# One hybrid attention and expert layer on one core: router logits inside the output projection, rows gathered per 32-slot block of an expert, two more weight buffers, and the heads' remainders on VectorE instead of GpSimd

## The reference, cut to what matters

```python
x = x + merged @ w_out[i]
h = rms_norm(x, ffn_norm[i])
group_logits = h @ w_group + b_group          # 4 groups, top 1
exp_logits   = h @ w_router + b_router        # 8 experts in each, top 2 in the group
# every token goes to 2 of 32 experts
hid = silu(xb @ w_gate[e]) * (xb @ w_up[e])   # 2048 -> 512
y   = hid @ w_down[e]                         # 512 -> 2048
x = x + weighted sum of the two experts' rows
x = x + sigmoid(rms_norm(x, ple_norm[i]) @ w_ple_gate[i]) * (p[i] @ w_ple_proj[i])
```

## Time and profile before

| | us |
|---|---|
| median of 3 runs | 2308.14 |
| lowest and highest | 2308.02, 2311.95 |
| profiled execution, its own time | 2307.7 |
| its span on the core | 2306.2 |
| mean granted TensorE clock | 0.926 of full |
| TensorE busy | 1815.4 (79%) |
| VectorE busy | 859.9 (37%) |
| ScalarE busy | 698.6 (30%) |
| GpSimd busy | 377.2 (16%) |
| DMA, mean over the span | 257 GB/s, 593 MB |

### The profile page before, as it was taken

How to read it: one execution, slowest core, us unless ns; L and a number is a source line. 1 busy time by engine, 2 the same in 40 slices (tenths; PEclk the granted TensorE clock), 3 DMA queues, 4 the chain that set the end, 5 groups by cost and what they waited for, 6 DMA issues and landing times.

```text
span 2306.2 us, 40236 instructions
## 1 busy us (share of the span) xinstructions
PE 1815.4 (79%) x17038; PEld 1428.8 (62%) x17039; DVE 859.9 (37%) x1284; ACT 698.6 (30%) x952; POOL 377.2 (16%) x120
## 2 busy tenths in 40 slices
PE   5899999999987999999896776665556566655689
PEld 5688888888875888888775443333333333333367
DVE  1454465435533454544445322222222122222264
ACT  3355455544554343334331110000000000000063
POOL 7454454535443000000001000000000000000000
PEclk9999999999998999999996898888898888889899
DMA  7444434443422555555571899999999999999973
GB/s 155 110 129 127 109 103 115 110 120 97 109 92 82 192 193 190 193 191 194 202 291 46 347 426 424 426 427 426 426 426 426 426 426 426 426 426 427 426 289 108
DMA packets 256837, 593.05 MB, mean 257 GB/s; under 512 B 29450, under 2 KB 168970, under 8 KB 223242
## 3 DMA queue, kind: packets, MB, share of 16 engines
q1 hardware_dynamic: 256778, 592.19, 68.8%
HBM read 590.06 MB, written 2.10 MB: 257 GB/s over the span
## 4 chain that ended last, share of the span: by engine, by line
PE 48%; DMA 36%; DVE 6%; ACT 4%; DVEq 2%; ACTq 2%; issue 1%; POOL 1%; SPq 0%
DMA ring<-in_w_e_down 34%; PE bank L662 20%; PE bank L469 12%; PE bank L870 4%; PE bank L812 3%; DVEq L1242 2%; DVE ring L1367 1%; PE bank L587 1%; DVE mo L1361 1%; ACT ring L924 1%; ACT wh L924 1%; DMA ring<-in_w_in 1%; ACT L924 1%; PE bank L787 1%; PE bank L590 1%
## 5 line engine op out<-in xcount | busy, mean ns | idle before, releaser
L787 PE MATMUL bank<-ring,mo 128*32 128x128 f32 x8192 | 327.8, 327 | 262.6 <-DMA ring<-in_w_e_gate 131.4
L787 PEld LDWEIGHTS bank<-ring,mo 128*32 128x32 f32 x8192 | 282.3, 132 | 345.5 <-DMA ring<-in_w_e_gate 167.5
L924 ACT ACTIVATE wh<-ring 128x2048 fp32r<-128x2048 f32 x156 | 298.5, 1913 | 266.6 <-DMA ring<-in_w_in 143.1
L405 POOL TENSOR_TENSOR wl<-ring,wh 128x2048 fp32r<-128x2048 f32 x68 | 314.3, 4632 | 312.5 <-ACT wh L924 312.5
L1609 DVE TENSOR_TENSOR x_tok<-x_tok,bank 128x512 f32<-128x512 f32 x256 | 158.7, 681 | 497.0 <-PE bank L776 497.0
L469 PE MATMUL bank<-xh,wh 128*128 128x256 f32 x1088 | 292.0, 304 | 9.0 <-POOL xl L411 9.0
L924 ACT ACTIVATE mo<-bank 128x256 f32<-128x256 f32 (+3 forms) x201 | 68.2, 348 | 749.7 <-PE bank L799 338.1
L469 PE MATMUL bank<-xl,wh 128*128 128x256 f32 x1088 | 274.1, 288 | 0.0
L1436 DVE TENSOR_TENSOR wl<-ring,wh 128x2048 fp32r<-128x2048 f32 x80 | 183.3, 2292 | 232.7 <-ACT wh L924 232.7
L469 PEld LDWEIGHTS bank<-xh,wh 128*128 128x128 f32 x1088 | 213.5, 196 | 15.9 <-POOL xl L411 9.2
L469 PEld LDWEIGHTS bank<-xl,wh 128*128 128x128 f32 x1088 | 214.2, 197 | 2.4 <-issue 1.9
(11 more groups left out here) (337 smaller groups left out, 2278.7 us busy)
## 6 DMA issues: line engine op xcount, KB each, us to landing
ring<-in_w_e_down SPq DMA_DIRECT2D x64, 2048.0 KB, 26.7
ring<-in_w_e_gate SPq DMA_DIRECT2D x64, 2048.0 KB, 24.0
ring<-in_w_e_up SPq DMA_DIRECT2D x64, 2048.0 KB, 26.1
ring<-in_w_in SPq DMA_DIRECT2D x116, 1024.0 KB, 5.5
ring<-in_w_out SPq DMA_DIRECT2D x16, 1024.0 KB, 5.2
ring<-in_w_ple_gate SPq DMA_DIRECT2D x8, 2048.0 KB, 14.5
ring<-in_w_branch_a SPq DMA_DIRECT2D x8, 1024.0 KB, 5.1
ring<-in_w_branch_b SPq DMA_DIRECT2D x8, 1024.0 KB, 5.2
```

The lines of the kernel that those rows point to most:

```text
L405: pool.tensor_tensor(wl[p][:], slot[p], wh[p][:], ALU.subtract).then_inc(sem("w_lo"), 1)
L787: m = mm(bank[b][32 * j:32 * j + 32, 0:P], xw[:, 8 * (i % 2) + k, :], m_gu[i][:, k, j * P:j * P + P], start=(i % 2 == 0 and k == 0), stop= ...
L924: return act.activation(out, in_, func, **kw)
```

## The change

1. **Remainders.** GpSimd keeps only the first two tiles' remainders and `xl`. All others go to VectorE, as `lo(p, t)`, one at a time at fixed places in its lists (in `mix` after `decT`, after `sp`, after `eG`, in rounds 1 and 3, before the chunks, in chunk 1, and after the head). The long stand of ScalarE in the last head is shortened: high parts of units 6 and 7 come after it.
2. **Start.** TensorE waits for `xh` instead of `xl`, products with `xl` come second in a tile; `gc` and the eight diagonal products go between head 0's dense quarters.
3. **Router logits.** While block n of the output projection runs, block n-1 of the new x is transposed, scaled by `ffn_norm` (`ngr`, a further small load) and multiplied with the router's weights; the root is applied to the logits afterwards. `h_tok` is made by ScalarE.
4. **Gather.** No `sel`, `xs`, `h_hi`, `h_lo`. Each window begins with eight float32 products of its own 32 selected slots (`selw`) with `h_rows`, an evacuation `xg`, four transposes and `xw`.
5. **Buffers.** The freed space makes two more gate buffers; gate pieces of even and odd experts alternate. Expert 1's gate pieces and `wpp` are loaded before the first window; loads of experts 0 and 1 start at units 78 to 84.

The diff, cut to its core:

```diff
-            base[f"plfull{b}"] = (f"mfull{b}", 16 * NE)
+            base[f"plfull{b}"] = (f"mfull{b}", 16 * (NE // 2 if b < 2 else NE))
...
+        xg = mo[:, 8192:8704]
+        x1T = [mo[:, 8192 + 1024 * i:9216 + 1024 * i].rearrange("p (k s) -> p k s", k=4) for i in range(2)]
...
+        m_flat += [xnT[:, :, :].rearrange("p t s -> p (t s)").rearrange("p (a n) -> p a n", a=1),
+                   mo[:, 4096:8192].rearrange("p (a n) -> p a n", a=1)]
...
+                if u in (78, 80):
+                    i = 4 + (u - 78) // 2
                     sp.wait_ge(*event("mT_lo", 8))
+                    expert_piece(i, 0).then_inc(sem(f"mfull{i}"), 16)
+                if u in (82, 84):
+                    i = (u - 82) // 2
+                    sp.wait_ge(*event("unit_mm", NG_U))
+                    expert_piece(i, 1, 1).then_inc(sem(f"mfull{i + 6}"), 16)
+            for i in (0, 2, 1, 3):
+                sp.wait_ge(*event("unit_mm", NU - 2 + 2 * (i % 2)))
                 expert_piece(i, 0).then_inc(sem(f"mfull{i}"), 16)
-            sp.wait_ge(*event("gathered", KT))
-            sp.dma_start(wpp[:], wpp_v).then_inc(sem("wpp_in"), 16)
-            with sp.Fori(1, NE) as e:
-                for i in range(6):
-                    sp.wait_ge(*event(f"mused{i}", e))
-                    expert_piece(i, e).then_inc(sem(f"mfull{i}"), 16)
+            sp.dma_start(wpp, wpp_v).then_inc(sem("wpp_in"), 16)
+            for i in range(2, 6):
+                sp.wait_ge(*event(f"mused{i}", 1))
+                expert_piece(i, 1).then_inc(sem(f"mfull{i}"), 16)
+            with sp.Fori(1, NE // 2) as h:
+                for odd in range(2):
+                    for i in range(6):
+                        sp.wait_ge(*event(f"mused{i}", 2 * h + odd - (1 if i < 2 else 0)))
+                        expert_piece(i, 2 * h + odd, odd).then_inc(sem(f"mfull{i + 6 * odd if i < 2 else i}"), 16)
...
-                steps = [(wh[p], x_, k) for k in range(KT) for x_ in (xh, xl)] + [(wl[p], xh, k) for k in range(KT)]
+                steps = [(w_, x_, k) for w_, x_ in ((wh[p], xh), (wh[p], xl), (wl[p], xh)) for k in range(KT)]
...
-            pe.wait_ge(*event("x_lo", 8))
+            pe.wait_ge(*event("x_hi", 8))
...
+            for q in range(4, 32):
+                dense(0, q)
+                if q % 2 == 1 and q // 2 - 2 < 8:
+                    i = q // 2 - 2
+                    pe.wait_ge(*event("diag", i + 1))
+                    if i >= 2:
+                        pe.wait_ge(*event("diag_bc", i - 1))
+                    mm(bank[4 + i % 2][:], ones[:], (cv if i % 2 == 0 else ex)[:, 0:512], start=True, stop=True)\
+                        .then_inc(sem("diag_mm"), 1)
...
-            pe.wait_ge(*event("head", NH + 1))
+            pe.wait_ge(*event("dn_ort", NH))
...
+                    if n and j == 1:
+                        x1_transposes(n - 1)
+                    if n and j == 2:
+                        part_logits(n - 1)
+            x1_transposes(3)
+            pe.wait_ge(*event("lT", 1))
             for t in range(TT):
+                pe.wait_ge(*event("x1T", 7 + t))
+                logits = bank[7][:, t * 36:t * 36 + 36]
+                mm(logits, lT[:, t * P:t * P + P], ident[0:NG + NE, 0:NG + NE], start=True, stop=False)
+                for k in range(4):
+                    m = mm(logits, x1T[1][:, k, t * P:t * P + P], wr[:, 12 + k, :], start=False, stop=(k == 3))
...
+            def window(v, gate_full, full, odd, last):
+                pe.wait_ge(*event("selw", v))
+                pe.wait_ge(*event("hidden", v))
+                for t in range(TT):
+                    for j in range(4):
+                        m = mm(bank[0][32 * j:32 * j + 32, :], selw[:, t, :], h_rows[:, t, 512 * j:512 * j + 512],
+                               start=(t == 0), stop=(t == 1))
+                m.then_inc(sem("xg_mm"), 1)
+                combine(v, 0).then_inc(sem("c_mm"), 1)
+                pe.wait_ge(*event("xg", v))
+                for q in range(4):
+                    m = pe.transpose(bank[1][:, q * P:q * P + P], xg[:, q * P:q * P + P], ident[:])
+                m.then_inc(sem("xw_mm"), 1)
                 pe.wait_ge(*event("xw", v))
...
-                if s in (2, 3, 5, 6, 7, 8):
+                if s in (2, 3, 5, 6):
                     unit_hi(s if s < 4 else s - 1)
             mix(NH, lambda s: None, first_units, lambda: None)
+            unit_hi(6)
+            unit_hi(7)
...
+            def lo(p, t):
+                dve.wait_ge(*event("w_hi", t + 1))
+                tt(wl[p][:], slot[p], wh[p][:], ALU.subtract).then_inc(sem("v_lo"), 1)
+            lo(2, 2)
+            lo(3, 3)
             dve.wait_ge(*event("small_in", 16 * SMALL))
...
                 tt(eG, eG, qk_dn[:, 0:S], ALU.mult).then_inc(sem("decays_used"), 1)
+                lo(4)
...
                     if r < 4:
                         next_tap(r)
+                    if r in (1, 3):
+                        lo(5 + r // 2)
...
                 next_silu()
+                lo(7)
                 for c in range(NCH):
...
+                    if c == 1:
+                        lo(8)
...
             def window(v, c):
-                dve.tensor_copy(xw, xs[:, :, ds(c, WIN)]).then_inc(sem("xw"), 1)
+                for t in range(TT):
+                    i = ts(selw[:, t, :], iota[:, ds(c, WIN)], pw[:, t:t + 1], None, ALU.is_equal)
+                i.then_inc(sem("selw"), 1)
                 add(v, 0)
+                dve.wait_ge(*event("xw_mm", v))
+                tt(xw.rearrange("p (j q) s -> p q j s", j=4), bank[1][:].rearrange("p (q j s) -> p q j s", q=4, j=4),
+                   bc(ngf[:].rearrange("p (j q) -> p q j", j=4).unsqueeze(3), [P, 4, 4, WIN]), ALU.mult)\
+                    .then_inc(sem("xw"), 1)
```

More of the change, by code:

```diff
@@ L787, in window @@
                             m = mm(bank[b][32 * j:32 * j + 32, 0:P], xw[:, 8 * (i % 2) + k, :],
-                                   m_gu[i][:, k, j * P:j * P + P], start=(i % 2 == 0 and k == 0),
+                                   m_gu[piece][:, k, j * P:j * P + P], start=(i % 2 == 0 and k == 0),
                                    stop=(i % 2 == 1 and k == 7))
@@ L823, in expert @@
                     with pe.Fori(0, more) as w:
-                        window(w0 + w + 1, e1 * 16, False)
-                window(w0 + more + 1, e1 * 16, True)
+                        window(w0 + w + 1, gate_full, full, odd, False)
+                window(w0 + more + 1, gate_full, full, odd, True)
             def ple_part(n):
@@ L835, in _ @@
             pe.wait_ge(*event("jobs", 1))
-            expert(0, 1)
+            pe.wait_ge(*event("h_tok", 2))
             pe.wait_ge(*event("pT", 1))
             pe.wait_ge(*event("wpp_in", 16))
-            ple_part(0)
-            with pe.Fori(1, 4) as e:
-                expert(e, e + 1)
-                ple_part(e)
-            with pe.Fori(4, NE) as e:
-                expert(e, e + 1)
+            with pe.Fori(0, 2) as h:
+                for odd in range(2):
+                    expert(h, odd)
+                    ple_part(2 * h + odd)
+            with pe.Fori(2, NE // 2) as h:
+                for odd in range(2):
+                    expert(h, odd)
             more = pe.value_load(jobs[0:1, 0, NE - 1:NE], min_val=0, max_val=7)
@@ L988, in _, with decay_rows @@
                 .then_inc(sem("gc_exp"), 1)
-            for i in range(0, 8, 2):
+            def decay_rows(i):
                 act.wait_ge(*event("diag_mm", i + 1))
@@ L1464, in x1_add, with x1_evac @@
                     tt(o, o, bank[2 * (n % 2) + t][:], ALU.add).then_inc(sem("x1"), 1)
+            def x1_evac(n):
+                for t in range(TT):
+                    dve.wait_ge(*event("x1T_in", 2 * n + t + 1))
+                    if n == 2:
+                        dve.wait_ge(*event("lT_part", 1))
+                    if n == 3:
+                        dve.wait_ge(*event("lT_part", 2))
+                    tt(x1T[n % 2][:, :, t * P:t * P + P], bank[4 + t][:].rearrange("p (k n) -> p k n", k=4),
+                       bc(ngr[:, 4 * n:4 * n + 4].unsqueeze(2), [P, 4, P]), ALU.mult).then_inc(sem("x1T"), 1)
             for b in range(3):
@@ L1477, in _ @@
                     x1_add((u - 79) // 4)
+                if u in (81, 85):
+                    x1_evac((u - 81) // 4)
                 unit_lo(u)
+            x1_evac(2)
             x1_add(3)
-            dve.wait_ge(*event("x1_rms", 1))
-            for t in range(TT):
-                ts(h_tok[:, t, :, :], x_tok[:, t, :].rearrange("p (c k) -> p k c", k=KT), rs2[:, 4 + t:5 + t], None,
-                   ALU.mult).then_inc(sem("h_tok"), 1)
-            evac_T(xnT, "hT", ngf)
+            x1_evac(3)
             dve.wait_ge(*event("logits", 1))
@@ L1489, in _ @@
             b8 = lambda i, w: bc(rsm[:, i, :].unsqueeze(2), [P, TT, w])
-            lp = bank[6][:, 0:72].rearrange("p (t n) -> p t n", t=TT)
```

(4 more changed lines are left out.)

217 lines of the change are left out of this document (98 added, 119 removed).

## The result

The changed kernel is slower: 2402.93 us (median of 4 runs, 2400.93 to 2411.28) beside 2309.1 (2308.02 to 2311.95), a ratio of 1.0411 (95% interval 1.0384 to 1.0439). Faster by 54 us was forecast. The profiled execution was the slowest of the four, with a span of 2409.3 us.

The account below looks back on a forecast made before the run. DMA was taken to bound the expert stage and TensorE nearly the heads, with a DMA hole between. Terms 1 to 5 summed as -8 +2 -8 +8 -47.5 = -53.5, thus 2254 us; range 2228 to 2282.

Parts of the forecast that it names:

- Term 5: Last output unit to expert 1's loads: first buffer free at U+40, +4 for early holes, later gather hidden; -47.5 us.
- three signs: Heads off by over 3 us each, a period above 29.5 after four experts, or TensorE awaiting DMA between output units.
- the rivals: Heads gain fully, 2216 us (0.10); early windows decide, 2271 (0.13); remainders on path, 2340 (0.04); DMA starts late, 2275 (0.02).
- the slower one: Seven loop heads: all 18.3 us of VectorE's remainders a head come on the path, +88 instead of +2, 2340 us; chance 0.04.
- Term 2: Seven loop heads: long VectorE rows vanish, new waits cost +6, steadier clock gives -4; +2 us in all.
- no wait of that length is left: -4: Seven loop heads: without the 3.3 us wait, the lower clock's loss of about 1 us in some heads goes.
- Terms 1, 3 and 4: Start, earlier dense tiles: -8 us; last head, gate products sooner: -8; output projection, added transposes and router products: +8.
- its 7 us: Early expert windows: the second, 3.4 us pause lowers the clock, costing 1.7 us more each, 7 in all, none later.

Follow-up runs that it names:

- one copy: Changed kernel with TensorE's second copy of the window code, for experts of more than one window, left out: 2263.93 us, 0.9804 of the kernel before.

## Why the prediction was wrong

The marks, in us; "heads" is from the second turn of the loop to the last head (VectorE's copy of `hs`), "branch" the first product with `oh`, U the end of the last output unit, "freed" SyncE's first load that waits for window 0, "last" the last half of the down products. "GpSimd" is one copy with the remainders back on GpSimd.

| stretch | before | changed | one copy | GpSimd | forecast |
|---|---|---|---|---|---|
| start to second turn | 211.37 | 207.32 | 204.26 | 204.91 | -8 |
| six turns | 456.4 | 467.4 | 464.2 | 458.2 | +2 |
| last head to branch | 89.5 | 80.2 | 80.0 | 78.6 | -8 |
| branch to U | 447.1 | 456.2 | 456.1 | 456.3 | +8 |
| U to freed | 77.4 | 40.8 | 37.3 | 37.4 | 40 |
| freed to last | 921.3 | 1054.4 | 912.3 | 915.5 | 911.2 |
| last to end | 103.2 | 103.0 | 103.0 | 103.0 | same |

**Term 5 failed, in its last part.** "Windows without `ple_part` need some 21 us of 29.5; there the gather is hidden under DMA" counted instructions and their durations, and not that the same loop was now twice as long in code. The 21 us were right (20.5 measured); the window began to cost more when it could no longer stay where TensorE runs it from. From the freed buffer to the last down products 1054.4 us passed instead of 911.2, and with one copy 912.3. The last down products came at 2306.3, 156.8 us after the forecast's 2149.5 (a span of 2252.7 less 103.2): 143.2 of it in this stretch, 12.8 up to U and 0.8 between. By the medians the code is worth 139. The rest of the term held: the buffer free at U+40.8 (forecast U+40; U+37.3 without a fetch ahead of window 0), and the last half at U+949.6 with one copy (forecast 951.2). Two of its figures don't follow from their own terms: 19.7, 2, 885 and 4 are 910.7 and not 911.2, and 24.45 with at most 2.0 and 3.4 is 29.9 and not 31.4. Neither matters beside 143.

Of the three signs I had named for a wrong forecast, one decided, "a period above 29.5 after the first four experts", and I had no mechanism for it. None of the rivals held it either: the slower one had its place in the heads. What was in sight before: the loops over experts in the diff, two experts a turn instead of one, and the number of packets on q8.

**Term 2 was mis-sized.** +2 for the heads; six turns measured +11.0 in the changed kernel and +7.8 with one copy. VectorE's long rows went, as forecast: the row that took 4.08 us is L1410, and it comes behind a remainder:

```profile
292.82 2.29 DVE L1303 TENSOR_TENSOR wl<-ring,wh 128x2048 fp32r<-128x2048 f32 x1 [0.52 <-ACT wh L955]
295.02 0.48 DVE L1410 SCALAR_TENSOR_TENSOR mo<-mo,gains,ring 128x256 f32<-128x256 f32 x1
```

With GpSimd subtracting again it is long again:

```profile
289.74 4.10 DVE L1413 SCALAR_TENSOR_TENSOR mo<-mo,gains,ring 128x256 f32<-128x256 f32 x1 [1.37 <-ACT ring L968]
```

```profile
288.94 14.04 POOL L435 TENSOR_TENSOR wl<-ring,wh 128x2048 fp32r<-128x2048 f32 x3 [13.14 <-ACT wh L968]
```

That agrees with the Trainium skill's rule on the shared port (SBUF — State Buffer, Who interferes with whom). And the new waits came nearly as listed. In one turn of the run with one copy:

```profile
PE bank L565 <- DVE ring L1444: 2.1, 1, 2.1
PE bank L615 <- DVE mo L1463: 1.6, 1, 1.6
PE bank L574 <- DVE ring L1450: 1.3, 2, 1.1
PE bank L515 <- ACT ring L952: 0.8, 1, 0.8
```

They sum to 5.8 us, where I had 6.6, and a turn at full clock takes 75.84 us, 0.6 over the 75.21 of before. What failed is "and no wait of that length is left: -4". The clock fell as often or more, and further (turns under 1.00: four of six before and with one copy, five of six in the changed kernel). Two turns of the run with one copy, whose waits are the same to a tenth:

```profile
204.26:283.15 78.89, 72.76 (x517) 66.99 (x516) 39.04 (x68) 39.82 (x64) 0.00 (x0) 0.96 0.40 106
...
360.58:436.42 75.84, 69.73 (x518) 64.31 (x517) 39.04 (x68) 39.90 (x64) 0.00 (x0) 1.00 0.42 111
```

A turn at 0.96 is 3 us longer than one at 1.00. With the remainders on VectorE the six turns with one copy ran at 0.96, 0.98, 1.00, 0.96, 0.98 and 1.00, and in the changed kernel one took 75.9 us and the others 77.3 to 79.0; before, one alone was at 0.96. Over six turns at full clock (451.3 before, 455.0 with one copy) the clock cost 5.1 us before, 9.2 with one copy and 12.4 in the changed kernel. So the +7.8 is 3.8 of work and waits, less than forecast, and 4.1 of clock where -4 had been taken. That share of the clock is not firm: the run with GpSimd subtracting, whose heads are those of before, lost 6.9 us to the clock where before lost 5.1, and the changed kernel 3.2 more than the same heads with one copy. Why the clock falls in one turn and not in the next with the same waits stays open, and so does whether this is all of the 8.9 us that GpSimd gave: the two profiled executions differ by only 3.2 of span, 6.0 gained in the six turns, 1.4 in the last head, 3.2 lost again in the loads.

**Terms 1, 3 and 4 held.** Dense tiles start at 67.98 (forecast 67), though the stretch, which holds a first turn of the heads too, gave 4 to 7 us of the 8. The last head gave 9.3 (8), and the output projection cost 9.1 (8).

**The Trainium skill's rule on the clock**, which I had weighed (TensorE: Matmul & The Clock Gate, HAM oscillation — how this bites in real kernels), bore on more than its 7 us. In the expert stage the clock was 0.77 with the pauses of the fetches and 0.88 without, and 0.96 where neither fetches nor weights made pauses. The lower clock came with the fetches; with one copy, at 0.88, the stage kept to DMA's 426 GB/s, so that the clock cost nothing there.

With the code kept small the measured span is 2257.2 against 2252.7 forecast (2254.2 less 1.5), and the median of 2263.9, 10 us above the forecast, lies inside the range that the changed kernel missed.

## What to carry to other kernels

Before a loop is written out to choose a buffer by parity, count its code, what is jumped over as well: every copy of the body, times the turns written out. In the profile, a packet count on the instruction queue that grows with the number of turns, and "issue" ahead of the same line in every turn, show a loop that is fetched anew; its price is hidden only as far as the loop waits for something else anyway. And when an engine's waits are exchanged for others of the same sum, look at the granted clock of each turn before calling it even.

## What had not been expected of the hardware

- A loop on TensorE of some 105 KB stays (44 packets in the whole run); one of some 122 KB is fetched anew in each turn, all of it (170). Sizes are estimates from the packets of 16 KB and the counts of instructions.
- Such a fetch stops TensorE for 6.9 and 3.0 us a turn with DMA at a share of 0.21, and for 12.1 and 4.9 while the DMA engines stream weights at 414 to 418 GB/s.
- Such fetches cost 25 us in one kernel and 139 in another, with 267 us (L787) and 193 us (L799, L813 and L790) of "issue" in the 700 us from 1400 on.
- Turns of a loop with the same waits ran at a clock of 0.96, 0.98 and 1.00, up to 3 us apart.
